# Attention with a forget gate: biases and causal masks added by VectorE from broadcast rows instead of by TensorE products

## The reference, cut to what matters

```
s = einsum('bqhd,bkhd->bhqk', q, k) * (FOX_HEAD_DIM ** -0.5)
s = s + cq[:, :, :, None] - ck[:, :, None, :]     # c: running sum of the log forget values, per head
s = where(kpos[None, :] <= qpos[:, None], s, -inf)
p = softmax(s, axis=-1)
o = einsum('bhqk,bkhd->bqhd', p, v)
```

## Time and profile before

| | us |
|---|---|
| runs of the kernel before (median of 3) | 1886.13 |
| lowest and highest run | 1880.18, 1888.01 |
| span of the profiled execution (first to last instruction) | 1885.1 |

### The profile page before, as it was taken

The page is one execution under the profiler, slowest core; times in us unless marked ns, Lnnn a source line. Parts: engine busy times, 40 slices in busy tenths (PEclk is TensorE's granted clock), DMA queues, the critical chain, the costliest instruction groups (busy, mean ns, idle before and its releaser), DMA issues.

```text
span 1885.1 us, 29064 instructions
## 1 busy us (share of the span) xinstructions
PE 1849.9 (98%) x12004; PEld 1642.4 (87%) x12004; DVE 983.0 (52%) x1569; ACT 722.0 (38%) x1144; POOL 225.9 (12%) x357
## 2 busy tenths in 40 slices
PE   8999999999999999999999999999999999999998
PEld 8777799998888887799998899998897777999986
DVE  4557653443567778743443664443465576543434
ACT  4246443333255454333332343333242463433321
POOL 3114070000011222230000100000031230000000
PEclk9999999999999999999999999999999999999999
DMA  7357254433353433444433434433364562444332
GB/s 246 128 203 229 81 160 123 129 129 123 117 164 105 125 116 104 118 139 125 124 134 123 146 101 125 132 124 125 110 206 150 200 221 90 137 132 124 128 129 79
DMA packets 179171, 259.38 MB, mean 138 GB/s; under 512 B 14717, under 2 KB 122349, under 8 KB 179040
## 3 DMA queue, kind: packets, MB, share of 16 engines
q1 hardware_dynamic: 161184, 197.18, 32.3%
q0 software_dynamic: 17856, 60.35, 9.9%
HBM read 243.19 MB, written 13.19 MB: 136 GB/s over the span
## 4 chain that ended last, share of the span: by engine, by line
PE 90%; DVE 4%; ACT 3%; issue 1%; DMA 1%; SPq 0%; DVEq 0%; ACTq 0%
PE ps L1605 14%; PE ps L1607 14%; PE ps L1606 14%; PE ps L1617 11%; PE ps L1615 11%; PE ps L1616 11%; PE ps L1833 1%; PE ps L1951 1%; PE ps L1938 1%; PE ps L1638 1%; PE ps L1888 1%; PE ps L1671 1%; DVE w_lo L785 1%; PE ps L1908 1%; PE ps L1673 1%
## 5 line engine op out<-in xcount | busy, mean ns | idle before, releaser
L785 DVE TENSOR_TENSOR w_lo<-w_raw,w_hi 128x1024 fp32r<-128x1024 f32 x370 | 452.1, 1228 | 709.1 <-ACT w_hi L439 707.9
L439 ACT ACTIVATE w_hi<-w_raw 128x1024 fp32r<-128x1024 f32 x370 | 389.3, 1059 | 803.5 <-DMA w_raw<-in_w_ffn_in_dram 363.1
L1605 PE MATMUL ps<-xT_hi,w_hi 128*128 128x384 f32 x1568 | 528.4, 337 | 2.5 <-issue 1.4
L1607 PE MATMUL ps<-xT_hi,w_lo 128*128 128x384 f32 x1568 | 527.0, 336 | 0.0
L1606 PE MATMUL ps<-xT_lo,w_hi 128*128 128x384 f32 x1568 | 526.9, 336 | 0.0
L1605 PEld LDWEIGHTS ps<-xT_hi,w_hi 128*128 128x128 f32 x1568 | 294.8, 188 | 5.2 <-issue 5.1
L1606 PEld LDWEIGHTS ps<-xT_lo,w_hi 128*128 128x128 f32 x1568 | 294.8, 188 | 0.1
L1607 PEld LDWEIGHTS ps<-xT_hi,w_lo 128*128 128x128 f32 x1568 | 294.8, 188 | 0.0
L1617 PE MATMUL ps<-w_hi,hT_lo 128*128 128x512 f32 x528 | 210.6, 399 | 0.0
L1616 PE MATMUL ps<-w_lo,hT_hi 128*128 128x512 f32 x528 | 208.1, 394 | 0.0
L1615 PE MATMUL ps<-w_hi,hT_hi 128*128 128x512 f32 x528 | 207.4, 393 | 0.0
(11 more groups left out here) (329 smaller groups left out, 2021.8 us busy)
## 6 DMA issues: line engine op xcount, KB each, us to landing
w_raw<-in_w_ffn_in_dram SPq DMA_DIRECT2D x352, 256.0 KB, 3.2
w_raw<-in_w_ffn_out_dram SPq DMA_DIRECT2D x176, 256.0 KB, 2.9
w_raw<-in_w_fox_in_dram SPq DMA_DIRECT2D x96, 256.0 KB, 2.9
k_c<-in_cache_fox_k_dram POOLq DMA_DIRECT2D x32, 512.0 KB, 5.3
v_c<-in_cache_fox_v_dram POOLq DMA_DIRECT2D x32, 512.0 KB, 4.0
w_raw<-in_w_hgrn_in_dram SPq DMA_DIRECT2D x64, 256.0 KB, 2.9
w_raw<-in_w_fox_out_dram SPq DMA_DIRECT2D x32, 256.0 KB, 2.9
out_dram<-kv_tok POOLq DMA_DIRECT2D x4, 1024.0 KB, 5.0
```

What stands on the lines that cost most here:

```text
L439: nc.scalar.activation(w_hi[:, slot, :], w_raw[:, slot, :], ACT.Copy).then_inc(hi_ready, 1)
L785: V.tensor_tensor(w_lo[:, slot, :], w_raw[:, slot, :], w_hi[:, slot, :].bitcast(F32), ALU.subtract).then_inc(lo_ready, 1)
L1605: mm(out, w_hi[:, slot, cols], x_hi[:, k, :], start=k == 0, stop=False, skip_group_check=True)
L1607: last = mm(out, w_lo[:, slot, cols], x_hi[:, k, :], start=False, stop=k == KD - 1, skip_group_check=True)
```

## The change

The products with the bias and the mask are taken out of `p_scores` and `s_pairs`, and with them `c_p`, `c_s`, `sel_p`, `sel_s`, `ident_r`, `causal_r` and what filled them. The running sums are stored to DRAM (`sums_p`, `sums_s`) by GpSimd's queue and loaded back broadcast over the query rows: `bias_p`, two heads for each load and two buffers, 128 x 768 elements (384 KB), and `bias_s`, one sample for each load and two buffers, 128 x 544 (272 KB). GpSimd subtracts the mask from each loaded bias in place (`mask_prompt_bias` over 128 x 512 elements, `mask_sample_bias` over 128 x 32). The first four loads and masks come before the loop; the other twelve are spread over it by `next_bias`, one in each turn: wait for the bias loaded the turn before, mask it, issue the next load.

The queries are scaled by -SCALE, so that scores are negative, and VectorE makes score + bias and its minimum in one instruction (`tensor_tensor_reduce`) into `p_s` or `p_p` in SBUF. ScalarE makes exp(-x + minimum) from SBUF in place. TensorE's `p_scores` and `s_pairs` wait for VectorE (`nmax`, `s_nmax`) where they waited for ScalarE's exponential.

```diff
+        sums_p = nc.dram_tensor("sums_p", [2, HEADS, T], F32)
+        sums_s = nc.dram_tensor("sums_s", [2, HEADS // 2, DB, 2, PAST + DT], F32)
...
 # ScalarE, fox
-                        act.wait_ge(*at(f["c_lo"], 3))
+                        act.wait_ge(*at(f["bias_in"], LOADED))
...
-                        nc.scalar.activation(p_s[:, (n - 1) % 2, :], ps[:, SS_BANK, 0:PAST + DT], ACT.Exp,
-                                             bias=nmx[:, (n - 1) % 2, 2:3], accum_out=rs[:, (n - 1) % 2, 2:3]).then_inc(f["s_exp"][0], 1)
+                        nc.scalar.activation(p_s[:, (n - 1) % 2, :], p_s[:, (n - 1) % 2, :], ACT.Exp,
+                                             bias=nmx[:, (n - 1) % 2, 2:3], scale=-1.0, accum_out=rs[:, (n - 1) % 2, 2:3]).then_inc(f["s_exp"][0], 1)
...
 # VectorE, fox
+                    if n == 0:
+                        dve.wait_ge(*at(f["bias_in"], LOADED))
...
-                        V.tensor_reduce(nmx[:, (n - 1) % 2, 2:3], ps[:, SS_BANK, 0:PAST + DT], AX_X, ALU.max,
-                                        negate=True).then_inc(f["s_nmax"][0], 1)
+                        if n % 2:
+                            dve.wait_ge(*at(f["bias"], sample_bias(n // 2)))
+                        V.tensor_tensor_reduce(out=p_s[:, (n - 1) % 2, :], in0=ps[:, SS_BANK, 0:PAST + DT],
+                                               in1=bias_s[:, (n - 1) // 2 % 2, (n - 1) % 2, :], scale=1.0, scalar=LARGEST, op0=ALU.add,
+                                               op1=ALU.min, accum_out=nmx[:, (n - 1) % 2, 2:3]).then_inc(f["s_nmax"][0], 1)
...
-                        V.tensor_reduce(nmx[:, n % 2, 0:1], ps[:, bank, 0:P], AX_X, ALU.max, negate=True)
-                        V.tensor_reduce(nmx[:, n % 2, 1:2], ps[:, bank, P:T], AX_X, ALU.max,
-                                        negate=True).then_inc(f["nmax"][0], 1)
+                        if n % 2 == 0:
+                            dve.wait_ge(*at(f["bias"], prompt_bias(n // 2)))
+                        for q, lo, hi in ((0, 0, P), (1, P, T)):
+                            ins = V.tensor_tensor_reduce(out=p_p[:, n % 2, lo:hi], in0=ps[:, bank, lo:hi],
+                                                         in1=bias_p[:, n // 2 % 2, n % 2, lo:hi], scale=1.0, scalar=LARGEST, op0=ALU.add,
+                                                         op1=ALU.min, accum_out=nmx[:, n % 2, q:q + 1])
+                        ins.then_inc(f["nmax"][0], 1)
...
 # GpSimd, fox: after the stores of the keys, before the loop
+                pool.wait_ge(*at(f["c"], 1 + DB))
+                pool.dma_start(sums_p[j, :, 0:P], cp[:, 0:P]).then_inc(f["bias_in"][0], 16)
+                pool.dma_start(sums_p[j, :, P:T], cp[:, :]).then_inc(f["bias_in"][0], 16)
+                for hf in range(2):
+                    pool.dma_start(sums_s[j, :, :, hf, :], craw[8 * hf:8 * hf + 8, :, :]).then_inc(f["bias_in"][0], 16)
+
+                def load_prompt_bias(k):
+                    pool.dma_start(bias_p[:, k % 2, :, :], sums_p[j, 2 * k:2 * k + 2, :].partition_broadcast(P)).then_inc(
+                        f["bias_in"][0], 16)
+
+                def load_sample_bias(b):
+                    pool.dma_start(bias_s[:, b % 2, :, :],
+                                   sums_s[j, :, b, :, :].rearrange("h f k -> h (f k)").unsqueeze(1).broadcast_to(
+                                       [HEADS // 2, DT, 2 * (PAST + DT)])).then_inc(f["bias_in"][0], 16)
+
+                def mask_prompt_bias(k):
+                    blocks = bias_p[:, k % 2, :, :].rearrange("p e (t c) -> p e t c", t=NTOK)[:, :, 0:NTOK:2, :]
+                    G.tensor_tensor(blocks, blocks, causal[:, :].unsqueeze(1).unsqueeze(1).broadcast_to([P, 2, 2, P]),
+                                    ALU.subtract).then_inc(f["bias"][0], 1)
+
+                def mask_sample_bias(b):
+                    new = bias_s[:, b % 2, :, PAST:]
+                    G.tensor_tensor(new, new, new_mask[:, :].unsqueeze(1).broadcast_to([P, 2, DT]), ALU.subtract).then_inc(
+                        f["bias"][0], 1)
+
+                def next_bias(m):
+
+                    if m:
+                        pool.wait_ge(*at(f["bias_in"], LOADED + 16 * (4 + m)))
+                        if m % 2:
+                            mask_prompt_bias(m // 2 + 2)
+                        else:
+                            mask_sample_bias(m // 2 + 1)
+                    if m < 2 * DB - 4 and m % 2 == 0:
+                        pool.wait_ge(*at(f["nmax"], m + 2))
+                        load_prompt_bias(m // 2 + 2)
+                    elif m < 2 * DB - 4:
+                        pool.wait_ge(*at(f["s_nmax"], m + 1))
+                        load_sample_bias(m // 2 + 2)
...
 # GpSimd, the loop, at the end of a turn
+                    if n - KV <= 2 * DB - 4:
+                        next_bias(n - KV)
...
 # TensorE, p_scores
                     if k:
-                            pe.wait_ge(*at(f["exp"], h - 1))
+                        pe.wait_ge(*at(f["nmax"], 2 * k))
-                        mm(out, sel_p[:, h:h + 1].broadcast_to([CROWS, P]), c_p[:, :], start=True, stop=False, skip_group_check=True)
-                        mm(out.rearrange("p (t c) -> p t c", t=NTOK)[:, 0:NTOK:2, :], ident_r[:, :],
-                           causal_r[:, :].rearrange("p (t c) -> p t c", t=NTOK)[:, 0:NTOK:2, :], start=False, stop=False,
-                           skip_group_check=True)
...
 # TensorE, s_pairs
                     if n:
-                        pe.wait_ge(*at(f["s_exp"], n))
+                        pe.wait_ge(*at(f["s_nmax"], n))
...
-                    mm(ps[:, SS_BANK, 0:PAST + DT], sel_s[:, n % 2, :], c_s[:, n // 2, :], start=False, stop=True,
-                       skip_group_check=True).then_inc(f["s_scores"][0], 1)
```

More of the change, by code:

```diff
@@ L43 @@
 MASKED = -1e30
+LARGEST = 3.0e38
 NEWTON = 3
@@ L68 @@
 LO_AT = {35: 0, 39: 1}
-CROWS = 64 + DT
-LAID = 17
+LAID = 4
+LOADED = 16 * 4
 KV = 3
@@ L126, in trunk_program @@
         causal = sb("causal", [P, P], after("ident"))
-        ident_r = sb("ident_r", [P, P], after("causal"), F32R)
-        causal_r = sb("causal_r", [P, T], after("ident_r"), F32R)
-        fold = sb("fold", [P, 4, DT], after("causal_r"))
-        half = sb("half", [P, 2], after("fold"))
+        fold = sb("fold", [P, 4, DT], after("causal"))
+        new_mask = sb("new_mask", [P, DT], after("fold"))
+        half = sb("half", [P, 2], after("new_mask"))
         own = sb("own", [P, 2, HD], after("half"))
@@ L285, in trunk_program @@
             "z": 1, "zma": 2, "ze": 1, "zl": 1, "lf": 3, "cT": 5, "cT_ev": 5, "kT_done": KD, "kT_a": KD, "scores": KD,
-            "ones": 1, "c": 1 + DB, "laid": LAID, "c_hi": 3, "c_lo": 3,
+            "ones": 1, "c": 1 + DB, "laid": LAID, "bias_in": LOADED + 16 * 2 * DB, "bias": 2 * DB,
             **{k: HEADS for k in ("nmax", "exp", "rcp", "scaled", "pT", "pT_ev", "rcs")},
@@ L308, in trunk_program, with prompt_bias, sample_bias @@
         S_BANK, PT_BANK, O_BANK, KT_BANKS, SS_BANK, SPT_BANK = (0, 1), 2, 3, 4, 6, 7
+        def prompt_bias(k):
+            return k + 1 if k < 2 else 2 * k + 1
+        def sample_bias(b):
+            return b + 3 if b < 2 else 2 * b + 2
         block = ctx.enter_context(nc.Block())
@@ L1362, in fox @@
+                pool.wait_ge(*at(f["bias_in"], LOADED))
+                for k in range(2):
+                    load_prompt_bias(k)
+                for b in range(2):
+                    load_sample_bias(b)
+                pool.wait_ge(*at(f["kT_a"], KD))
+                pool.wait_ge(*at(f["bias_in"], LOADED + 16 * 4))
+                for k in range(2):
+                    mask_prompt_bias(k)
+                for b in range(2):
+                    mask_sample_bias(b)
                 pool.wait_ge(*at(f["kstored"], 16 * 2))
@@ L1887, in p_scores @@
                             rows = slice(HD * e, HD * e + HD)
-                            last = mm(ps[:, S_BANK[e], lo:hi], qz[rows, e, k, lo:lo + P], kT[rows, k, 0:n], start=False, stop=hi == T,
+                            last = mm(ps[:, S_BANK[e], lo:hi], qz[rows, e, k, lo:lo + P], kT[rows, k, 0:n], start=True, stop=True,
                                       skip_group_check=True)
@@ L1937, in s_pairs @@
                         rows, k = slice(32 * g, 32 * g + 32), 4 * (n % 2) + g
-                        mm(ps[rows, SS_BANK, 0:PAST + DT], qs[:, k, n // 2, :, :].rearrange("p e q -> p (e q)"), ktc[:, g, :],
-                           start=True, stop=False, skip_group_check=True)
-                    mm(ps[:, SS_BANK, 0:PAST + DT], sel_s[:, n % 2, :], c_s[:, n // 2, :], start=False, stop=True,
-                       skip_group_check=True).then_inc(f["s_scores"][0], 1)
+                        last = mm(ps[rows, SS_BANK, 0:PAST + DT], qs[:, k, n // 2, :, :].rearrange("p e q -> p (e q)"), ktc[:, g, :],
+                                  start=True, stop=True, skip_group_check=True)
```

(1 more changed line is left out.)

85 lines of the change are left out of this document (28 added, 57 removed).

## The result

The changed kernel takes 1903.9 us (median of 4 runs, 1902.81 to 1908.85) against 1885.43 us (now four runs, 1880.18 to 1888.01) for the kernel before: ratio 1.0102, 95% interval 1.0081 to 1.0122. It is 18.5 us slower, above the range of 1869 to 1893. The profiled execution has a span of 1901.3 us and took 1903.07.

A forecast was written before the change was run, and what follows sets the result against it. TensorE, busy 98%, was taken as near balance with a chain through other engines in the attention loop. Turns -13.3 and mask hits +3.2 gave -10.1: span 1885.1 to 1875.0, median 1876.0 us, range 1869 to 1893.

The forecast's parts named there:

- GpSimd's wait for bias loads under 1 us a turn: Sign to look for in the attention loop if the forecast held: GpSimd waits under 1 us a turn for bias loads.
- rival D: GpSimd's loop: each landing (L) waited for, other loads queued behind; break-even L 4.65, at 5.3 1901.7 us; chance 0.17.
- The gain that D had to eat: Loop gain per layer that GpSimd's landing waits had to use up before the kernel became slower: 6.6 us.
- the lead: Head start of GpSimd's bias loads, issued three turns ahead: some 6.3 us.
- The turn: Attention loop: odd and even turns both become bound by the chain, 4.35 us each where 4.54 and 4.99 alternated.
- The gain of -13.3: Attention loop: 0.83 us gained a pair of turns, 8 pairs in each of 2 layers, -13.3 us.
- the two unknown prices: Per turn: 0.10 us delay for each fused operation and 0.03 us for ScalarE's exponential reading SBUF.
- the foretold idle time of TensorE before `s_turn`: Sign in both kinds of turn: TensorE idle 0.2 to 0.4 us before `s_turn`.
- The fused operation: VectorE's addition with minimum: 0.45 to 0.5 us over 272 columns plus a short second instruction; 0.10 us delay each.
- rival C: Gain eaten on VectorE: all 12 masks hit (1882.4), or fused operation at the scan's rate (about 1883); chance 0.28.
- The masks: GpSimd's prompt masks stall VectorE's scaling in the loop: 2 hits in 6 a layer at 0.8 us, +3.2 us.
- 326 of 332 GB/s: DMA queue in the loop: data and bias loads ask for 326 GB/s each 4.35 us, against 332 if full.

The follow-up runs named there:

- h1_waitonly: Changed kernel with its loads, load order and GpSimd's landing waits kept but no masks; VectorE waits for the landing itself: 1898.12 us, ratio 1.0074.
- e3_nomask: Changed kernel with all loads but no masks in the loop; VectorE waits for landings, GpSimd only two turns later: 1880.92 us, ratio 0.9981.
- h2_smallloads: Changed kernel with all waits, masks and orders, but each bias load in the loop brings an eighth of its columns: 1879.93 us, ratio 0.9973.
- e5_masksonly: Changed kernel with the masks in the loop but without the bias loads and their waits: 1877.77 us, ratio 0.9957.
- e6_noproducts: Kernel before the change with the bias and causal products left out and nothing in their place: 1874.99 us, ratio 0.9938.
- e2_noloads: Changed kernel with no bias loads, waits or masks in the loop; the first four biases are reused: 1873.3 us, ratio 0.993.
- f2_sp_masks: Complete changed kernel with the twelve loop loads issued by SyncE's queue; GpSimd still waits for each landing and masks it: 1885.39 us, ratio 0.9997.
- f1_sp_nomask: Changed kernel without masks in the loop, its twelve loop loads issued by SyncE's queue: 1883.98 us, ratio 0.9994.

## Why the prediction was wrong

**The step that failed** is a term that the sum did not have. The loop was costed as turns of TensorE, VectorE and ScalarE, with a correction for masks; GpSimd's wait for each landing stood in it at nothing ("GpSimd's wait for bias loads under 1 us a turn"). It measured 26.6 us in the first loop, 2.2 us for each of 12 loads. `h1_waitonly` against `e3_nomask` prices it at 17.2 us with no mask about. Its mechanism was on paper as rival D, with 0.17, and the range stopped at 1893 although D's own time, 1901.7, stood beside it; that is 2.2 us below the measured 1903.9, and that near by luck (below).

**Why D was held for unlikely.** The reason given was that a bias that is waited for stands behind little in its queue. In the changed kernel the wait itself bunches the key, value and new-value loads behind it, and the next bias follows them within 6 us; in `h2_smallloads`, where the prompt's follows the keys by 2 to 3 us, even 48 KB take 5.2. The landing rows (3.9, 4.0, 5.3) were spread around the 4.65 at which D broke even, and that alone spoke for more than 0.17.

**D's own terms: the formula right, the nearness of its time luck.** The period 2L + 1.30 + 0.25 holds: the masks' starts from 144.93 to 199.53 us are five periods of 10.9, which is L = 4.7; in layer 3 they are 11.2. But D took L = 5.3 for all six pairs. From the first load's issue to the last mask's end (137.18 to 205.43), with the slow first landing of 7.7 us in it, are 68.25 us, six periods of 11.4 and L = 4.9: 16.0 us more than six pairs of 8.7, where D had 20.7. The gain that D had to eat was taken as 6.6 us a layer; with masks it is 4.0 (71.1 - 67.1 in `e5_masksonly`). And 16.0 less the 4.0 and the 6.7 that layer 0 really lost leaves 5.3 for the lead, where D had 6.3. So 20.7 - 6.6 - 6.3 = 7.8 stands for 16.0 - 4.0 - 5.3 = 6.7: a landing that was too dear against a gain and a lead that were too large. Layer 3 lost 9.3 us, 2.8 of them by the clock, which no theory had.

**The turn: the length right, by two errors that cancel.** 4.35 us was predicted for both kinds, 4.33 measured; TensorE's removed 19.9 us bring about 10 (`e6_noproducts`), for the reason given, that the products were the cover of the chain. The gain of -13.3 is -12.2 in `e2_noloads`. The bare turn is 4.30 where 4.22 was worked out from the rows of before, and the two unknown prices together are 0.03 us where 0.13 was taken. The missing 0.08 us lie on a path that was left out. The fold's weights wait for `x_s`, as before the change, and load at S+0.69; ScalarE copies the fold's result at S+1.16, in its order ahead of the exponential. Before, the exponential came later anyway. In `e6_noproducts` (S = 170.57) it starts behind this copy, 0.55 us after the maximum (171.30), not 0.48:

```profile
171.73 0.22 ACT L594 ACTIVATE xT_hi<-ps 128x64 fp32r<-128x64 f32 x1
171.85 0.48 ACT L599 ACTIVATE p_s<-ps,nmx 128x272 f32<-128x272 f32 x1
```

The same wait makes TensorE's own work up to `s_turn`, put at 1.59 us, as long as the chain (`s_turn` starts at S+1.91). So the foretold idle time of TensorE before `s_turn` shows in no product's row; only the weight load of `s_turn` waits, 0.33 us for `p_s`.

**The fused operation: too dear.** It takes 442 ns over 272 columns, to the nanosecond the maximum's time; the extremum is indeed fetched by a second instruction, 84 ns, but it starts 0.37 us after the first, under it. By form, busy us and mean ns:

```profile
L1008 DVE CUSTOM_DVE_ANT_0 p_s<-ps,bias_s 128x272 f32<-128x272 f32 x16 | 7.1, 442 | 10.4 <-POOL bias_s L1374 9.4 <-PE ps L1977 0.3
L1036 DVE CUSTOM_DVE_ANT_0 p_p<-ps,bias_p 128x256 f32<-128x256 f32 x16 | 6.6, 415 | 0.0
...
L1008 DVE DVE_READ_ACCUMULATOR2_ANT nmx<- 128x1 f32 x16 | 1.3, 84 | 0.0
```

The two instructions are what the Trainium skill, "VectorE: DVE Perf Modes", says of an accumulator output; the trace agrees (a second instruction of 84 ns), and adds that it costs nothing here. The halved throughput that rival C named is not there with one source in PSUM; whether the operation, CUSTOM_DVE_ANT_0 in the trace, belongs to the family meant there, no run shows.

**The masks: the mechanism right, the size in two wrong parts.** 2 hits in 6 at 0.8 us gave +3.2. With no landing to wait for (`e5_masksonly`), every mask meets the scaling and costs 0.37 to 0.4 us, not 0.8, since the turn after gets part back: +4.5. The Trainium skill, "SBUF — State Buffer", section "Who interferes with whom", has the port between these two engines as an exclusive lock; 1.64 us where the scaling takes 0.55 in the turn beside it agrees with it. In the changed kernel landings come late, and only three of 12 masks hold a scaling for long (1.34, 1.56 and 1.43 us at 156.0, 1520.7 and 1543.1), near the 4 that were forecast. Between `h1_waitonly` and the changed kernel stand 5.8 us, 3.9 by the turns of the profiled executions. 2.8 of these are the fallen clock, which the loops of `h1_waitonly` don't show; the masks' 1.5 us in each of 12 periods of GpSimd's own loop may be a part of the rest, which was not tried.

**The bytes: seen and not priced.** 326 of 332 GB/s stood under D only. By themselves they cost 7.6 us (`e3_nomask`), with no wait of GpSimd for a landing in its first loop. Even without D the sum would have been about 1873.3 + 4.5 + 7.6, 1885.4: no change, as `f2_sp_masks` measured, though with its two prices divided otherwise.

## What to carry to other kernels

A wait for a landing in the instructions that issue all loads puts that landing into the period of every load; write that loop out as period = landings + work, with everything that stands ahead of the load in it, compare it with the turn before giving it a small chance, and let the stated range reach as far as the rival does. Products that are removed from TensorE are worth only what their cover was not: find the chain that ends last without them (here 4.30 us), and ask of each single product what waits under it. Here the DMA share stood at 0.8, and a third more bytes had a price of their own, whoever issued them.

## What was not expected of the hardware

- A small load lands hardly sooner than a large one from the same place behind large transfers: 7.1 us for 48 KB, 7.7 for 384 KB, as first load of the loop. After a pause of the queue 34 KB take 2.9 us.
- The fused add and minimum, with its fetch, is as fast as a plain maximum (442 ns for 272 columns); the exponential over 272 columns reads SBUF in 0.52 us for 0.49 from PSUM.
- A stall can be followed by a slow stretch that costs on top of it. In the changed kernel's layer 3 TensorE stood 1.72 us before 1528.07 and 2.76 us before 1551.40, and each time the granted clock then fell from 1.00 to the lower level (0.50, 1.2 GHz) for some microseconds. The transposes of `s_keys` took 1.90 us in the first, for 1.04 a turn later, and from `s_turn` to the next S passed 3.98 and 3.61 us, for 2.40 at full clock: 2.8 us in all. In `f1_sp_nomask` the same followed 2.22 us before 161.93. In layer 0 of the changed kernel waits as long (1.76 us before 163.45, 2.40 before 185.41) were followed by no fall; what decides it, these runs don't show. The mean granted clock is 0.994 to 0.996 in the changed kernel's four executions and 0.996 to 0.999 in those of the variants, which speaks for such falls in each of the four. Windows of 2 us of the changed kernel (the granted clock is the third value from the end):

```profile
1527.00:1529.00 2.00, 0.93 (x6) 0.91 (x7) 1.75 (x10) 0.93 (x3) 2.00 (x4) 0.86 0.92 329
1529.00:1531.00 2.00, 2.00 (x14) 1.67 (x16) 0.61 (x1) 0.77 (x2) 0.30 (x1) 0.50 0.56 120
1531.00:1533.00 2.00, 1.91 (x34) 1.32 (x34) 0.85 (x5) 1.63 (x6) 1.24 (x2) 0.78 0.94 350
1533.00:1535.00 2.00, 2.00 (x19) 1.55 (x19) 1.67 (x10) 1.12 (x4) 2.00 (x4) 1.00 0.59 190
```
